# The compress product's high and low token blocks as one 64-column stationary operand

## The reference

```python
n_cmp = (T - CMP_LEN) // CMP_STRIDE + 1          # T 256, CMP_LEN 32, CMP_STRIDE 16: 15 blocks
def compress(x, pe, w1, w2):                     # once for keys, once for values
    blk = x[:, cmp_idx] + pe[None, None, :, None, :]
    blk = jnp.transpose(blk, (0, 1, 3, 2, 4)).reshape(B, n_cmp, G, CMP_LEN * Dh)   # G 2 groups, 32 * 64 = 2048
    hid = jax.nn.gelu(jnp.einsum('bngi,ih->bngh', blk, w1))                        # w1: 2048 x 256
    return jnp.einsum('bngh,ho->bngo', hid, w2)
```

## Time and profile before

| | |
|---|---|
| time, median of 3 runs | 1664.19 us |
| lowest and highest of them | 1661.94 and 1666.49 us |
| profiled execution, span from first to last instruction | 1662.6 us |
| mean granted TensorE clock in it | 0.993 of full |
| the two layers of the second kind, about | 1316 to 1487 and 1487 to 1656 us of the span |

### The profile page before, as it was taken

The page is one execution under the profiler, slowest core; times in us unless marked ns, Lnnn a source line. Parts: engine busy times, 40 slices in busy tenths (PEclk is TensorE's granted clock), DMA queues, the critical chain, the costliest instruction groups (busy, mean ns, idle before and its releaser), DMA issues.

```text
span 1662.6 us, 27116 instructions
## 1 busy us (share of the span) xinstructions
PE 1611.2 (97%) x11156; PEld 1454.2 (87%) x11156; DVE 1065.9 (64%) x1269; ACT 825.5 (50%) x1123; POOL 264.3 (16%) x208
## 2 busy tenths in 40 slices
PE   7999999999999999999999999999999999999997
PEld 7999888888989998999988888999999887879885
DVE  4655557665765455555565766566555679867985
ACT  5443446653454433543454665335443556655563
POOL 0000060010000000000034000000000069306940
PEclk9999999999999999999999999999999999999999
DMA  7757555333546655555746444255565455155612
GB/s 226 224 183 232 176 179 167 121 127 102 173 157 203 200 178 177 181 187 191 231 158 195 127 145 128 102 178 169 186 200 178 135 185 194 33 157 165 218 33 89
DMA packets 206612, 273.97 MB, mean 165 GB/s; under 512 B 18774, under 2 KB 167096, under 8 KB 206008
## 3 DMA queue, kind: packets, MB, share of 16 engines
q1 hardware_dynamic: 206376, 272.67, 51.2%
q10 hardware_dynamic: 144, 0.00, 0.0%
HBM read 271.61 MB, written 1.08 MB: 164 GB/s over the span
## 4 chain that ended last, share of the span: by engine, by line
PE 83%; DVE 11%; ACT 2%; issue 2%; POOL 1%; DMA 0%; SPq 0%; POOLq 0%; ACTq 0%; DVEq 0%
PE bank L503 29%; PE bank L550 14%; PE bank L985 8%; PE bank L974 7%; PE bank L1175 4%; DVE wlo L435 2%; PE bank L2037 2%; PE bank L2286 2%; PE bank L1257 2%; PE bank L2015 1%; PE bank L1118 1%; PE bank L956 1%; PE bank L1093 1%; ACT whi L424 1%; PE bank L2122 1%
## 5 line engine op out<-in xcount | busy, mean ns | idle before, releaser
L435 DVE TENSOR_TENSOR wlo<-raw,whi 128x2048 fp32r<-128x2048 f32 (+1 forms) x258 | 584.0, 2268 | 335.6 <-ACT whi L424 335.0
L424 ACT ACTIVATE whi<-raw 128x2048 fp32r<-128x2048 f32 (+1 forms) x258 | 484.1, 1880 | 319.6 <-PE bank L550 101.4
L503 PE MATMUL bank<-hT_hi,whi 128*128 128x256 f32 x1408 | 395.7, 281 | 0.8 <-DVE hT_lo L354 0.3
L503 PE MATMUL bank<-hT_lo,whi 128*128 128x256 f32 x1408 | 394.2, 280 | 0.0
L503 PE MATMUL bank<-hT_hi,wlo 128*128 128x256 f32 x1408 | 394.1, 280 | 0.0
L503 PEld LDWEIGHTS bank<-hT_hi,whi 128*128 128x128 f32 x1408 | 266.3, 189 | 3.5 <-issue 0.9
L503 PEld LDWEIGHTS bank<-hT_lo,whi 128*128 128x128 f32 x1408 | 266.4, 189 | 1.4
L503 PEld LDWEIGHTS bank<-hT_hi,wlo 128*128 128x128 f32 x1408 | 266.3, 189 | 0.0
L550 PE MATMUL bank<-whi,Y 128*128 128x512 f32 x704 | 223.9, 390 | 0.0
L308 POOL TENSOR_TENSOR st<-st 128x1 f32<-128x1 f32 x18 | 17.6, 980 | 938.8 <-ACT X L301 938.8
L550 PEld LDWEIGHTS bank<-whi,Y 128*128 128x128 f32 x704 | 132.2, 188 | 26.8
(11 more groups left out here) (396 smaller groups left out, 2822.6 us busy)
## 6 DMA issues: line engine op xcount, KB each, us to landing
raw<-in_ffn_w SPq DMA_DIRECT2D x132, 1024.0 KB, 5.5
raw<-in_w_in SPq DMA_DIRECT2D x80, 1024.0 KB, 5.5
raw<-in_w_out SPq DMA_DIRECT2D x16, 1024.0 KB, 4.9
raw<-in_w_br_na SPq DMA_DIRECT2D x4, 1024.0 KB, 6.0
raw<-in_w_br_mla SPq DMA_DIRECT2D x4, 1024.0 KB, 5.1
raw<-in_w_br_gla SPq DMA_DIRECT2D x4, 1024.0 KB, 5.0
raw<-in_cmp_k_w SPq DMA_DIRECT2D x4, 1024.0 KB, 6.4
raw<-in_cmp_v_w SPq DMA_DIRECT2D x4, 1024.0 KB, 5.2
```

What stands on the lines that cost most here:

```text
L424: act.activation(m["whi"][:, slot, 0:w], m["raw"][:, slot, 0:w], ACT.Copy).then_inc(s.hi_ready, 1)
L435: dve.tensor_tensor(m["wlo"][:, slot, 0:w], m["raw"][:, slot, 0:w], m["whi"][:, slot, 0:w].bitcast(F32), ALU.subtract).then_inc(s.lo_ready, 1)
L503: mm = pe.matmul(B[bank][:, mt * T:(mt + 1) * T], a, b, start=(n == 0 and k == 0), stop=(n == KK - 1 and k == 2))
```

## The change

The high and the low block of a slice are laid side by side, so that one stationary operand of 64 columns holds both. Two passes, by `whi` and by `wlo`, take the place of three; they give all four products of parts, of which the high block's fall on partitions 0 to 31 of the bank and the low block's on 32 to 63. VectorE adds the two halves: a copy of the low block's sums out of PSUM to SBUF, then an add of the high block's, in the place of one copy. Since the 16 slices of a block now lie at one even distance, `block_high` and `block_low` write them with two instructions of 240 numbers in place of four of 120.

```diff
-    blk_s = lambda v, part, j: Y[:, 8 + 2 * v + j // 8, part, (j % 8) * 32:(j % 8) * 32 + 32]
+    blk_runs = Y[:, 8:12, :, :].rearrange("p a b c -> p (a b c)").rearrange("p (v j n) -> p v j n", v=2, j=16)
+    blk_s = lambda v, j: blk_runs[:, v, j, :]
+    blk_part = lambda v, part, g: blk_runs[:, v, :, 32 * part + 16 * g:32 * part + 16 * g + N_CMP]
...
@@ w1 (TensorE)
                 j = 8 * (i % 2) + j8
-                left = (blk_s(v, 0, j), blk_s(v, 1, j))
-                for k, (a, b) in enumerate(passes(left, ring.w(slot, j8 * 256, 256))):
-                    mm = pe.matmul(B[6][0:32, v * T:(v + 1) * T], a, b, start=(j == 0 and k == 0), stop=(j == 15 and k == 2))
+                for k, b in enumerate(ring.w(slot, j8 * 256, 256)):
+                    mm = pe.matmul(B[6][0:64, v * T:(v + 1) * T], blk_s(v, j), b, start=(j == 0 and k == 0),
+                                   stop=(j == 15 and k == 1))
...
@@ block_high (ScalarE)
-            for q in range(2):
-                dst = Y[:, 8 + 2 * v + q, 0, :].rearrange("p (j g n) -> p j g n", j=8, g=2)
-                for g in range(2):
-                    ins = act.activation(dst[:, :, g, 0:N_CMP], blk[:, v, 8 * q:8 * q + 8, g, 0:N_CMP], ACT.Copy)
+            for g in range(2):
+                ins = act.activation(blk_part(v, 0, g), blk[:, v, :, g, 0:N_CMP], ACT.Copy)
...
@@ block_low (VectorE)
-            for q in range(2):
-                for g in range(2):
-                    hi, lo = (Y[:, 8 + 2 * v + q, part, :].rearrange("p (j g n) -> p j g n", j=8, g=2)[:, :, g, 0:N_CMP]
-                              for part in range(2))
-                    ins = TTo(lo, blk[:, v, 8 * q:8 * q + 8, g, 0:N_CMP], hi.bitcast(F32), ALU.subtract)
+            for g in range(2):
+                ins = TTo(blk_part(v, 1, g), blk[:, v, :, g, 0:N_CMP], blk_part(v, 0, g).bitcast(F32), ALU.subtract)
...
@@ gelu (VectorE)
-            h = B[6][0:32, v * T:(v + 1) * T]
+            h, by_low = (B[6][32 * part:32 * part + 32, v * T:(v + 1) * T] for part in range(2))
...
-            chain(dve.tensor_copy(f, h))
+            chain(dve.tensor_copy(t_, by_low))
+            chain(TTo(f, t_, h, ALU.add))
```

## The result

| | before | changed |
|---|---|---|
| time, median (16 runs each) | 1664.55 us | 1667.34 us |
| lowest and highest | 1661.94 and 1667.81 us | 1664.48 and 1670.33 us |
| ratio, with its 95% interval | | 1.0016 [1.0009, 1.0022] |
| profiled execution, span | 1662.6 us | 1668.4 us |
| mean granted TensorE clock in it | 0.993 | 0.988 |

The changed kernel takes 2.7 us more (1.5 to 3.7). The forecast was 1665.5 us, +1.3 us, no change within 0.3%. That there would be no change, and the range, held; the size was off by a factor of two. The profiled execution of the changed kernel was the slowest of the sixteen: its time was 1670.33 us, 3.0 above the median (a run's time lies 1.8 to 1.9 us above its span in most runs).

A forecast was written before the change was run, and what follows sets the result against it. VectorE's queue was taken to bound the stretch, hiding TensorE's saved passes. Adds of 0.96 less block_low's 0.3 gave +0.66 us a layer, +1.3 in two: span 1663.9, with 1.6 around it 1665.5 us; range 1660.5 to 1669.5.

The forecast's parts named there:

- The passes: Compress product on TensorE: 64 passes of 0.115 us removed, 7.4 us in all, none of it on the path.
- The waits: TensorE's waits for VectorE: 3.25 and 1.65 us at scores.0, 2.7 at turn.0, about 1.2 at tok_b.1.
- block_low: VectorE's pairs ahead of fox_bias: 1.89 us falls to 1.6, saving 0.3 a layer; ends 0 and 0.6.
- The covering engine: Around the w1 units, VectorE's queue was said to hide all 7.4 us removed from TensorE.
- If that cover were gone up to 7.4 us would come off: Around the w1 units, without VectorE's queue as cover, the removed TensorE passes could gain up to 7.4 us.
- The add: One more chained VectorE instruction per gelu: 0.48 us each, 0.96 a layer, fully on the path.
- the low end: The add in gelu priced like the PSUM copy, 0.44 us each, 0.88 a layer.
- The upper end, 1.66: Both gelu adds of a layer priced from the long L2635, 0.80 us plus 0.03 hand-over each.
- the slower rival: TensorE's clock falls in longer gaps at scores.0 and turn.0, 3.4 us a fall, up to 1672.3 us; chance 0.09.
- If the clock row shows new stretches at 0.50: Sign of error: TensorE granted half clock, 1.2 in place of 2.4 GHz, in new places.
- 1672 us for two falls: Clock falls at both turn.0 gaps add 6.8 us to 1665.5, giving 1672.3 us.
- The likeliest sum: On VectorE, 0.96 for adds less 0.3 for smaller block copies: +0.66 us a layer, +1.3 in two.

The follow-up runs named there:

- e4: Changed kernel without the add: gelu copies only the high block's sums; 1664.13 us, ratio 1.0005 to before.
- e5: Changed kernel with idle matmuls ahead of scores.0 (24) and turn.0 (16); 1667.05 us, ratio 1.0023 to before.
- e11: Changed kernel with VectorE's convolution steps taps.1 to taps.7 left out; 1664.10 us, ratio 0.9989 to before.
- e2: Kernel before with one more chained VectorE instruction, the add's size, in each gelu; 1667.69 us, ratio 1.0028.
- e8: Changed kernel with the copy of the low block's sums moved from VectorE to ScalarE; 1665.64 us, ratio 1.0012 to before.
- e3: Kernel before with the new token block layout and two-instruction block_high and block_low, but three passes and old gelu; 1663.19 us, ratio 1.0002.
- the second set: Changed kernel run again unedited, on another chip than the first runs of the experiments; 1667.21 us, ratio 1.0024 to before.
- e10: Kernel before with VectorE's convolution steps taps.1 to taps.7 left out; 1665.47 us, ratio 1.0000.
- e6: Kernel before with idle matmuls (11 and 8) ahead of cmp_score's two waits; 1659.48 us, ratio 0.9982.
- e1: Changed kernel with a third pass put back, the low part of w1 taken twice; 1669.51 us, ratio 1.0036 to before.
- e12: Kernel before with the new layout, two-instruction block_high and block_low, and idle matmuls ahead of cmp_score's waits; 1661.64 us, ratio 0.9980.

## Why the prediction was right, and where it was not

**The passes: right.** 0.117 us each against 0.115, and none of the 7.4 us on the path (e4: 1.0005). The waits stand where they were put: scores.0 3.62 against 3.25 us, the second layer's 2.35 against 1.65 (VectorE came later there, see block_low), turn.0 3.22 and 3.00 against 2.7, tok_b.1 1.22 against 1.2 where the clock kept up (e5).

**The covering engine: right in before, too strong as a statement.** "VectorE's queue is the bound and TensorE follows it" holds for the kernel as it was. "If that cover were gone up to 7.4 us would come off" was not borne out: e11 lost the cover and gained 1.4 us, if that. A wait of 0.38 us at turn.0 should have been read as two queues of almost one length.

**The add: the mis-sized term.** Itself it took 0.41 us, as the low end had it. The sum then treated VectorE's successors as fixed. They are not: with the start of the chain shifted by 0.44 us, two instructions of 0.41 and 1.22 us met GpSimd's adds and became 0.83 and 1.76, less 0.30 us for three others. The term measured 1.43 us a layer (e2, second layer; 1.44 in e5's first) in place of 0.96, so 2.9 in two. The upper end, 1.66, held it by luck: it had priced the add as the one that waits.

By the Trainium skill, "SBUF — State Buffer", section "SBUF: two separate sides", an operation of VectorE with two SBUF inputs and one of GpSimd exclude each other for the whole instruction. The traces agree for the add, which reads PSUM and took 0.41 us at most in every run, in e8 (1393.67, 0.40 us) all of it inside an add of GpSimd's, and for its successors in SBUF beside GpSimd's add. They show a limit too: beside GpSimd's scalar multiplication prob.0's second half took its usual time in all 18 cases, and L2515, which began just behind one, was some 0.25 us longer but did not wait for its end.

**block_low: the saving came, the gain did not.** The pairs take 0.92 + 0.71 = 1.63 us against 1.6 forecast, from 1.89. But fox_bias's last instruction ends at 1363.41 against 1363.33: L2508 and L2510 grew by 0.55 and 0.38 us, both in a meeting with GpSimd's add. The term was 0 (e3: 1.0002), the end given, in place of -0.3 us a layer, and in the second layer it was about 0.3 us the other way (77.09 against 76.78 us from ln.2 to scores.0).

**The clock: the slower rival's mechanism happened, and its price did not.** "If the clock row shows new stretches at 0.50" was named as a sign of error, and they are there, behind scores.0 and turn.0. In the first layer they cost 1.49 us ahead of turn.0 and 1.03 behind it (15.97 against 14.94). What the rival left out is that a fall moves the ones behind it: in the changed kernel the fall at cmp_score is gone from the first layer, and 2.79 and 1.49 us of the loss come back by ln.2. The exchange is not even in the profile: up to the kernels' last 5 us the changed one has 37 us at half clock, before 20, and 2.87 of its 5.8 us lie at the new stretch near 1492 us. In the timed runs, though, the falls at scores.0 and turn.0 filled (e5) or not, the ratio stays. So 1672 us for two falls was too much, and nothing for them in the likeliest case was right by luck, through an exchange that the prediction did not see.

**The total.** The likeliest sum was 1.3 us. With the terms as the rows give them it is 2 x 1.43 + 0 = 2.9 us; measured were 2.7 (1.5 to 3.7) and, in the second set, 4.0 (2.5 to 5.5). That 2.9 comes so near 2.7 proves little: the add alone, timed as a whole, cost 4.7 (2.8 to 6.5), and what the falls of the clock add or give back in all is open within a microsecond or two.

## What to carry to other kernels

Time taken from the busiest engine is worth what its next wait says: with a wait of 0.4 us at the end of the stretch, relieving one of the two engines gave nothing (e4, e10). That relieving both would was not shown (e11). An instruction added to a chain of VectorE's beside which GpSimd is busy is priced with its successors, by asking which of them will meet GpSimd's adds; putting it on an engine with room (here ScalarE) avoids that. Where an idle gap of TensorE is followed by a half clock, idle matmuls in the gap can be a cheap gain (e6), but look at the gaps behind it: a fall cured in one place can come back in the next (e5). Count the matmuls by the shortest wait, or they run past it.

## What the runs showed of the hardware

- A fall of TensorE's clock moves. Filling two gaps (e5) kept 1.00 there, and about 10 us at 0.50 stood behind the third, where the changed kernel had none; filling the third alone in before (e6) took 2.7 us off each layer.
- A gap of about 3.6 us with almost nothing to do was followed by half clock in each of the five kernels that had one ahead of scores.0. Of those with 2.55 to 2.81 us there, some fell (e1, e2, e12) and some did not (before, e3, e6, e10). A gap with 0.35 us of work in 3.00 fell as well. The length alone doesn't decide: in the second layer the gaps of 2.27 to 2.43 us ahead of scores.0 fell in the same five kernels.
- GpSimd's add of 128x256 held VectorE's instructions up until its end, and was itself stretched from 0.74 to 3.15 us beside a low part of VectorE that began 0.27 us after it (1352.05, beside L435 from 1352.32). Even L2508, which reads one tensor, was held, 0.82 in place of 0.27 us. GpSimd's scalar multiplication left prob.0's second half at its usual 1.21 us (18 of 18), while L2515, 0.08 us behind one, took 0.67 in place of 0.41.
- A stationary operand of 64 columns loads in 0.134 us, between 0.108 for 32 and 0.188 for 128, and the pass of 256 moving columns costs the same for all.
